# Where an expert's down weights are rounded, and how the second copy of the expert sums is added

## The chip, the cores and the metric

The kernel runs on one core of one Trainium2 chip. The metric is the device time of one execution in microseconds; lower is better. An execution of the kernel is profiled once beside the timed runs, and all rows below come from that one execution.

## What is computed

One encoder block over 1024 positions of 1024 channels: a token mixing part (spatial gating and a Fourier mix), then a mixture of experts, then a final norm. The change touches the expert part and the end. Cut to what matters:

```python
def step(y, blk):                       # one block: up to 128 rows of one expert
    tok, gate, e = blk
    xb = x_pad[tok]                     # 128 x 1024
    h = silu(xb @ w_gate[e]) * (xb @ w_up[e])      # 128 x 256
    out = (h @ w_down[e]) * gate[:, None]          # 128 x 1024
    return y.at[tok].add(out), None
y, _ = lax.scan(step, y0, blocks)       # 64 experts, top 8 of them for each of 1024 rows
h = h + routed + shared
return rms_norm(h, final_norm_g)
```

Everything is float32. Each expert brings 3 MB of weights (gate, up and down, 1 MB each).

## The kernel before

The rows that an expert has to work on are cut into **items** of 128 rows; the inputs here give 93 items for 64 experts, and experts with two items mostly alternate with experts that have one. Items run one after the other, three to a pass of the loop (`TURN = 3`).

Products are made with rounded operands in two parts: a weight tile is split into a **high** part (rounded by ScalarE, ACT: `split_gu` and `split_dn`, lines 959 and 963) and a **rest** (what is left, taken off by VectorE, DVE: `rest_gu` and `rest_dn`, lines 1203 and 1210). Three products of the parts then stand for one. Gate and up weights are split in two pieces (`GU_PARTS = 2`, one is gate and one is up, 128x2048 each), down weights in two of 128x1024 (`KF = 2`). Activations are split in the same way: `xTh` and `xTl` from the transposed rows, `hTh` and `hTl` from the transposed middle rows.

What TensorE (PE) does in item i, in order: the 8 transposes of item i+1's rows (L464), the 12 down products of item i-1 (L744, which need its `w_dn` and `hTl`), 2 transposes of item i's middle rows (L752, which need `hh`), and the 24 gate and up products of item i+1 (L730, which need `w_gu`, `xTh` and `xTl`). I give times in an item from its **T**, the start of its L464 transposes; the last of the 24 products is followed at once by the next T.

What ACT does in item i: the silu `hs` (L969), `xTh` (L974), the first piece of the gate and up weights for item i+2 if that item opens a new expert, `hTh` (L984), the copy `ob` of item i-1's result (L980), the second piece, and last the down weights for item i+1 if that item opens an expert. DVE: `hh` (L1367), `xTl` (L1374), the rest of item i's own down weights (ACT has rounded them one item before), `hTl` (L1379), and both gate and up rests for item i+2. An expert's weights are split once, in the items around its first block; the flags `now`, `coming` and `ahead` say whether item i, i+1 or i+2 is such a first block.

Loads are issued by SyncE (SP) from one instruction stream. There are two raw buffers for gate and up and two for down, one expert in each:

```python
load_next_gu(t * 2 + 1, 0)     # waits until expert j-2 is split on ACT and DVE, then issues
gu_landed(1, t + 1)            # waits for the other buffer's load, then tells ACT (s_rg)
load_next_dn(t * 2, 1)
dn_landed(0, t)                # tells ACT of down weights (s_rd)
```

So the word that expert j-1's gate and up weights have landed comes to ACT only behind the issue of expert j's load, which waits for expert j-2's split to be done.

Results of items are added to rows in HBM with an indirect accumulating DMA from GpSimd (POOL, L1583), in two copies, `yv` and `yv2`. The last three items are not stored: at the end their rows are added by one-hot products (L786). For the end, SP loads the first copy in 8 chunks of 128 rows into `ya_in` (L452), and POOL adds the second copy to each chunk with an accumulating DMA (L1642). DVE then adds the one-hot products to a chunk (L1457, two halves), ACT squares it, POOL makes the root, DVE scales it (L1467), and SP stores it (L455).

Of the kernel before, what the change touches and what calls it, by code (L numbers as in the profile page):

```python
# [23 lines left out]
P = 128  # L24
D = 1024
# [37 lines left out]
def build(nc, x, g1, w_in, ln_g, ln_b, wsT, bsT, ga, gb, w_out, g2, w_router, rbias, wg, wu, wd,  # L63
          sg, su, sd, dft_pos, dft_ch, gf, out, hn_d, y_d):
    ctx = ExitStack()
    with ctx:
        top = [nc.sbuf_base]

        def place(name, shape, dt, at=None):
# [6 lines left out]
            if at is None:  # L76
# [136 lines left out]
        ob_rest = [place("ob_rest0", [P, D], F32R, Z_AT + 12 * KB), place("ob_rest1", [P, D], F32R, S_AT + 12 * KB),  # L213
                   place("ob_rest2", [P, D], F32R, T_AT)]
        tok_row = place("tok_row", [P, S], F16, M_AT + KB)
# [57 lines left out]
        s_yl = [sem(f"y_last_in{c}") for c in range(NC)]  # L273
        s_oh, s_obh, s_obl = sem("onehot_ready"), sem("last_results_high"), sem("last_results_rest")
        s_tok, s_col = sem("token_row"), sem("last_slot_columns")
        s_lastmm, s_sum = sem("last_rows_done"), sem("last_rows_added")
# [51 lines left out]
        def _(sp):  # L328
# [122 lines left out]
            for c in range(NC):  # L451
                sp.dma_start(ya_in[:, c, :], yv[c]).then_inc(s_x[c], 16)  # L452
            for c in range(NC):
                sp.wait_ge(s_of, c + 1)
                sp.dma_start(out_v[c], ya_in[:, c, :]).then_inc(s_ost, 16)  # L455
# [370 lines left out]
        def _(act):  # L826
# [166 lines left out]
            def item(i, u, turn, coming, final=False):  # L993

                silu(i)
                if final:
                    if u + 1 < TURN:
                        evac_xT(i + 1)
                    evac_h(i)
                    evac_out(i - 1, (u - 1) % TURN, turn if u else turn - 1)  # L1000
# [18 lines left out]
                with act.If(coming[0] > 0):  # L1019
                    act.wait_ge(s_rd, coming[1] + 1)  # L1020
                    split_dn(coming[2])
                return ahead

            def turn_of_items(turn, final=False):
                coming = expert(turn * TURN + 1)
                for u in range(TURN):
                    coming = item(turn * TURN + u, u, turn, coming, final and u > 0)
# [32 lines left out]
        def _(dv):  # L1060
# [327 lines left out]
            def item(i, u, now, coming, final=False):  # L1388
# [14 lines left out]
                if isinstance(i, int) and i == 0:  # L1403
# [47 lines left out]

            def add_last(c):
                dv.wait_ge(s_yl[c], 16)
# [5 lines left out]

            add_last(0)  # L1460
            add_last(1)
            dv.wait_ge(s_gf, 16)
# [9 lines left out]
        def _(gp):  # L1472
# [162 lines left out]
            for c in range(NC):  # L1635
                gp.wait_ge(s_x[c], 48)
                if c == 0:
# [61 lines left out]
```

## Time and profile before

| | us |
|---|---|
| median of 3 runs | 1382.69 (1381.22 to 1388.32) |
| the profiled execution, device time | 1384.51 |
| span of the profiled execution, first to last instruction | 1382.8 |
| PE busy | 1321.7 (96%) |
| DVE busy | 859.0 (62%) |
| ACT busy | 722.8 (52%) |
| POOL busy | 521.9 (38%) |

The profiled execution took 1.8 us more than the median, and 1.7 us of its device time lie around the span. About 900 us of the span are the expert loop, and the last 50 us or so are the end. A share of busy time is an average over stages; what bounds one stage is read from its waits.

### The profile page before, as it was taken

The numbers are of one execution on the slowest core, as the hardware profiler recorded it, in microseconds if no ns is written. First come the engines' busy times: TensorE is split into PE (matmuls) and PEld (weight loads), VectorE is DVE, ScalarE is ACT, GpSimd is POOL, SyncE is SP. The second block draws the span as 40 slices with busy tenths as digits, with TensorE's granted clock in tenths as the row PEclk, the third lists the DMA queues.
The fourth block names the chain that finished last, engine by engine and source line by source line (L and its number), as shares of the span: only waits on it lengthen the run. The fifth ranks groups of instructions, "written<-read, shape, count | busy, mean of one in ns | idle before, by whom it ended". The sixth has DMA issues, their size and how long they took to land.

```text
span 1382.8 us, 25986 instructions
## 1 busy us (share of the span) xinstructions
PE 1321.7 (96%) x6030; PEld 1033.6 (75%) x6032; DVE 859.0 (62%) x1203; ACT 722.8 (52%) x916; POOL 521.9 (38%) x610
## 2 busy tenths in 40 slices
PE   6999988999999999999999999999999999999996
PEld 5885465888445787888878887888778888888875
DVE  5430544355585667667766767667676767667766
ACT  5320244211002667676766657676666766676752
POOL 2431201000002444545444444444454444444562
PEclk9999998999899999999999999999999999999998
DMA  9604032011046799999999999999999999999979
GB/s 338 190 13 164 0 121 92 31 46 46 9 183 217 258 313 345 282 325 305 334 299 326 314 297 350 287 337 315 313 315 320 315 337 308 298 332 306 334 213 249
DMA packets 88306, 338.02 MB, mean 244 GB/s; under 512 B 12496, under 2 KB 23760, under 8 KB 71504
## 3 DMA queue, kind: packets, MB, share of 16 engines
q1 hardware_dynamic: 60624, 250.53, 47.2%
q0 software_dynamic: 27648, 87.06, 27.8%
q8 instruction: 18, 0.29, 0.1%
q14 instruction: 16, 0.13, 0.0%
HBM read 288.99 MB, written 65.27 MB: 256 GB/s over the span
## 4 chain that ended last, share of the span: by engine, by line
PE 57%; DVE 9%; DMA 9%; issue 9%; ACT 5%; SPq 5%; DVEq 4%; ACTq 1%; POOL 0%; POOLq 0%
PE ps L730 18%; PE ps L615 7%; PE ps L481 7%; PE ps_out L744 6%; DMA raw_dn<-in_w_down 5%; DVE w_gu L1203 5%; PE ps L650 4%; PE ps L517 4%; PE ps L464 4%; SPq L318 3%; DMA ya_in<-y_rows_dram 2%; ACT w_gu L959 2%; DVE w_dn L1210 2%; PE ps L566 2%; DVEq L318 2%
## 5 line engine op out<-in xcount | busy, mean ns | idle before, releaser
L730 PE MATMUL ps<-w_gu,xTh 128*128 x1488 | 468.6, 396 | 17.8 <-DVE xTl L1374 15.5
L730 PEld LDWEIGHTS ps<-w_gu,xTh 128*128 128x128 f32 x1488 | 273.8, 188 | 81.4 <-issue 27.1
L1583 POOL DMA_INDIRECT y_rows_dram<-ob,idxs x90 | 222.3, 2470 | 235.2 <-ACT ob L980 213.7
L1203 DVE TENSOR_TENSOR w_gu<-raw_gu,w_gu (+1 forms) x128 | 290.4, 2287 | 11.9 <-issue 11.8
L730 PE MATMUL ps<-w_gu,xTl 128*128 x744 | 291.1, 391 | 0.0
L959 ACT ACTIVATE w_gu<-raw_gu (+1 forms) x128 | 245.7, 1920 | 70.8 <-SPq L404 70.8
L744 PE MATMUL ps_out<-w_dn,hTh 128*128 x744 | 242.1, 407 | 1.6 <-ACT ob L980 1.6
L963 ACT ACTIVATE w_dn<-raw_dn (+1 forms) x128 | 128.2, 1053 | 87.3 <-SPq L408 78.4
L730 PEld LDWEIGHTS ps<-w_gu,xTl 128*128 128x128 f32 x744 | 139.7, 188 | 28.3
L1374 DVE TENSOR_TENSOR xTl<-ps,xTh 128x512 fp32r<-128x512 f32 x186 | 119.8, 686 | 59.5 <-ACT xTh L974 58.2
L744 PEld LDWEIGHTS ps_out<-w_dn,hTh 128*128 128x128 f32 x744 | 133.2, 189 | 27.0 <-issue 1.9
L1210 DVE TENSOR_TENSOR w_dn<-raw_dn,w_dn (+1 forms) x128 | 150.4, 1216 | 1.8 <-ACT w_dn L963 1.8
L744 PE MATMUL ps_out<-w_dn,hTl 128*128 x372 | 146.0, 392 | 0.0
L1557 POOL DMA_INDIRECT Xg<-hn_rows_dram,idxg x94 | 100.2, 1066 | 76.5 <-POOL idxg L1554 74.4
L974 ACT ACTIVATE xTh<-ps 128x512 fp32r<-128x512 f32 x186 | 101.3, 602 | 39.5 <-PE ps L464 39.5
L1367 DVE SCALAR_TENSOR_TENSOR hh<-hs,gate,ps 128x256 f32<-128x256 f32 x93 | 44.4, 477 | 119.9 <-ACT hs L969 119.9
L1505 POOL TENSOR_SCALAR rs<-ms 128x1 f32<-128x1 f32 x40 | 21.1, 527 | 230.4 <-ACT junk L829 229.2
L464 PEld LDWEIGHTS ps<-ident,Xg 128*128 128x128 f32 x744 | 96.9, 190 | 8.0 <-issue 0.5
L1567 POOL COPY gate<-Xg 128x1 f32 x93 | 41.1, 442 | 159.9 <-DVE hh L1367 102.2
L464 PE MATMUL ps<-ident,Xg 128*128 128x128 f32 x744 | 97.3, 274 | 0.0
L980 ACT ACTIVATE ob<-ps_out 128x1024 f32<-128x1024 f32 x92 | 94.1, 1023 | 0.0
L1379 DVE TENSOR_TENSOR hTl<-ps,hTh 128x256 fp32r<-128x256 f32 x93 | 39.0, 419 | 84.9 <-ACT hTh L984 84.9
(241 smaller groups left out, 1608.0 us busy)
## 6 DMA issues: line engine op xcount, KB each, us to landing
raw_gu<-in_w_gate SPq DMA_DIRECT2D x64, 1024.0 KB
raw_gu<-in_w_up SPq DMA_DIRECT2D x64, 1024.0 KB
raw_dn<-in_w_down SPq DMA_DIRECT2D x64, 1024.0 KB
y_rows_dram<-zero SPq DMA_DIRECT2D x1, 4608.0 KB, 20.0
x_ring<-in_x SPq DMA_DIRECT2D x8, 512.0 KB, 4.7
w_in_sb<-in_w_in SPq DMA_DIRECT2D x8, 512.0 KB, 9.9
xh<-in_x SPq DMA_DIRECT2D x8, 512.0 KB, 7.3
w_out_sb<-in_w_out SPq DMA_DIRECT2D x1, 4096.0 KB, 13.1
```

The lines of the kernel that those rows point to most:

```text
L464: last = pe.transpose(ps[banks[k // 4]][:, (k % 4) * P:(k % 4 + 1) * P], src[:, k:D:KD], ident[:, :])
L481: mm = pe.matmul(ps[2 + 2 * (c % 2) + half][:, :], x_[:, c % 2, k, :], w_, start=(k == 0 and n == 0), stop=(k == KD - 1 and n == 2))
L730: mm = pe.matmul(ps[3][:, :], x_[:, k, :], w_gu[:, bass.ds(at, 1), part, :, k, :], start=(k == 0 and part == 0 and x_ is xTh), stop=(k == ...
L744: mm = pe.matmul(ps[6 + half][:, :], h_[:, k, :], w_dn[:, bass.ds(at, 1), part, k, half * 512:(half + 1) * 512], start=(k == 0 and part == ...
L959: act.activation(gu_part(w_gu[:, :, 0, :, :, :], at, m), gu_part(raw_gu, at, m), ACT.Copy).then_inc(s_hg, 1)
L963: act.activation(w_dn[:, bass.ds(at, 1), 0, k, :], raw_dn[:, bass.ds(at, 1), k, :], ACT.Copy).then_inc(s_hd, 1)
L974: act.activation(xTh[:, half * 4:half * 4 + 4, :], ps[1 + half][:, :].rearrange("p (k t) -> p k t", k=4), ACT.Copy).then_inc(s_xa, 1)
L1203: dv.tensor_tensor(gu_part(w_gu[:, :, 1, :, :, :], at, m), gu_part(raw_gu, at, m), gu_part(w_gu[:, :, 0, :, :, :], at, m).bitcast(F32), AL ...
L1210: dv.tensor_tensor(w_dn[:, bass.ds(at, 1), 1, k, :], raw_dn[:, bass.ds(at, 1), k, :], w_dn[:, bass.ds(at, 1), 0, k, :].bitcast(F32), ALU.s ...
L1374: dv.tensor_tensor(xTl[:, part, :], ps[1 + half][:, :].rearrange("p (k t) -> p k t", k=4), xTh[:, part, :].bitcast(F32), ALU.subtract).the ...
L1557: gp.indirect_dma_start(out=Xg[:, u, :], out_offset=None, in_=hn_d[:, :], in_offset=bass.IndirectOffsetOnAxis(ap=idxg[:, u:u + 1], axis=0) ...
L1583: gp.indirect_dma_start(out=y_d[:, :], out_offset=bass.IndirectOffsetOnAxis(ap=idxs[:, u:u + 1], axis=0), in_=ob[:, u, :], in_offset=None, ...
```

## The change

In the expert loop, on ACT an item now rounds **its own** down weights (flag `now`) where it opens an expert, between the copy `ob` and the second piece of gate and up; before, the down weights of the next item (`coming`) were rounded at the item's end. On DVE the first gate and up rest now comes right behind `xTl`, ahead of `hTl`; then `hTl`, the down rest, and the second gate and up rest.

At the end, the second copy of chunks 0 to 3 is loaded by SP as a plain load into a new tile `yb_in`, in the place of the raw down weights, and added to `ya_in` by DVE (`both_copies`); POOL adds chunks 4 to 7 only. The tile `ob_rest0` moves out of the way of `yb_in`.

```diff
@@ SP, the end
             for c in range(NC):
                 sp.dma_start(ya_in[:, c, :], yv[c]).then_inc(s_x[c], 16)
+            sp.wait_ge(s_hd, NE * KF)
+            sp.wait_ge(s_ld, NE * KF)
+            for c in range(NC // 2):
+                sp.dma_start(yb_in[:, c, :], yv2[c]).then_inc(s_x[c], 16)
@@ ACT item
                 if not (isinstance(i, int) and i == 0):
                     evac_out(i - 1, (u - 1) % TURN, turn if u else turn - 1)
+                if not (isinstance(i, int) and i == 0):
+                    with act.If(now[0] > 0):
+                        act.wait_ge(s_rd, now[1] + 1)
+                        split_dn(now[2])
                 with act.If(ahead[0] > 0):
                     split_gu(ahead[2], (1,))
-                with act.If(coming[0] > 0):
-                    act.wait_ge(s_rd, coming[1] + 1)
-                    split_dn(coming[2])
@@ DVE item
                 else:
+                    with dv.If(ahead[0] > 0):
+                        rest_gu(ahead[2], ahead[1], (0,))
+                    rest_h(i)
                     with dv.If(now[0] > 0):
                         rest_dn(now[2], now[1])
-                if not (isinstance(i, int) and i == 0):
-                    rest_h(i)
-                with dv.If(ahead[0] > 0):
-                    rest_gu(ahead[2], ahead[1], range(GU_PARTS))
+                    with dv.If(ahead[0] > 0):
+                        rest_gu(ahead[2], ahead[1], (1,))
@@ DVE, the end
+            def both_copies(c):
+                dv.wait_ge(s_x[c], 64)
+                dv.tensor_tensor(ya_in[:, c, :], ya_in[:, c, :], yb_in[:, c, :], ALU.add).then_inc(s_both, 1)
...
+            both_copies(0)
+            both_copies(1)
             add_last(0)
+            both_copies(2)
             add_last(1)
+            both_copies(3)
@@ POOL, the end
-            for c in range(NC):
+            for c in range(NC // 2, NC):
                 gp.wait_ge(s_x[c], 48)
```

The order on ACT in one item of the loop, before (the branches skip a split where its flag is not set):

```order
L984 ACTIVATE hTh<-ps 128x256
L980 ACTIVATE ob<-ps_out 128x1024
L1017 COMPARE_AND_BRANCH
L959 ISA x2
L959 ACTIVATE w_gu<-raw_gu 128x2048
L1017 UNCONDITIONAL_BRANCH
L1019 COMPARE_AND_BRANCH
L1020 ISA
L963 ISA
L963 REGISTER_ALU
L963 ACTIVATE w_dn<-raw_dn 128x1024
```

and now:

```order
L992 ACTIVATE hTh<-ps 128x256
L988 ACTIVATE ob<-ps_out 128x1024
L1027 COMPARE_AND_BRANCH
L1028 ISA
L971 ISA
L971 REGISTER_ALU
L971 ACTIVATE w_dn<-raw_dn 128x1024
...
L1030 COMPARE_AND_BRANCH
L967 ISA x2
L967 ACTIVATE w_gu<-raw_gu 128x2048
```

The two down pieces moved from behind the second gate and up piece to ahead of it, and belong to the item itself. On DVE, in one item before:

```order
L1374 TENSOR_TENSOR xTl<-ps,xTh 128x512
L1410 COMPARE_AND_BRANCH
L1209 ISA
L1210 ISA x2
L1210 TENSOR_TENSOR w_dn<-raw_dn,w_dn 128x1024
...
L1379 TENSOR_TENSOR hTl<-ps,hTh 128x256
L1414 REGISTER_ALU
L1414 COMPARE_AND_BRANCH
L1202 ISA
L1203 ISA x2
L1203 TENSOR_TENSOR w_gu<-raw_gu,w_gu 128x2048
```

and now:

```order
L1384 TENSOR_TENSOR xTl<-ps,xTh 128x512
L1422 REGISTER_ALU
L1422 COMPARE_AND_BRANCH
L1212 ISA
L1213 ISA x2
L1213 TENSOR_TENSOR w_gu<-raw_gu,w_gu 128x2048
L1422 UNCONDITIONAL_BRANCH
L1389 TENSOR_TENSOR hTl<-ps,hTh 128x256
...
L1220 TENSOR_TENSOR w_dn<-raw_dn,w_dn 128x1024
...
L1213 TENSOR_TENSOR w_gu<-raw_gu,w_gu 128x2048
```

One gate and up piece moved ahead of `hTl`, and the down rests now stand behind it, ahead of the second piece.

## Rows read from the trace of the kernel before

**Rows 1.** The waits of all engines, 450 to 1322 us: total, times, longest
```profile
ACT w_gu L959 <- SPq L404: 70.8, 34, 4.2
PE ps L730 <- DVE xTl L1374: 15.5, 27, 1.3
```

**Rows 2.** The same view for SP's own queue, 450 to 1322 us
```profile
SPq L391 <- DVE w_gu L1203: 169.0, 61, 7.2
...
SPq L404 <- DMA raw_gu<-in_w_up: 6.9, 2, 6.7
```

**Rows 3.** Busy time by window: us, PE, PEld, DVE, ACT, POOL, clock, DMA share, GB/s
```profile
1200.00:1300.00 100.00, 98.59 (x478) 81.43 (x477) 71.25 (x72) 68.51 (x82) 47.73 (x52) 1.00 1.00 323
```

**Rows 4.** Timeline of PE, starts of items (T): start us, us, engine line op
```profile
466.79 0.93 PE L464 MATMUL ps<-ident,Xg 128*128 128x128 f32 x7
...
631.60 1.04 PE L464 MATMUL ps<-ident,Xg 128*128 128x128 f32 x8
...
640.99 1.05 PE L464 MATMUL ps<-ident,Xg 128*128 128x128 f32 x8
...
650.45 1.04 PE L464 MATMUL ps<-ident,Xg 128*128 128x128 f32 x8
...
654.96 0.50 PE L730 MATMUL ps<-w_gu,xTh 128*128 x1 [0.44 <-issue]
...
660.53 1.05 PE L464 MATMUL ps<-ident,Xg 128*128 128x128 f32 x8
...
1330.74 0.71 PE L464 MATMUL ps<-ident,Xg 128*128 128x128 f32 x5
```

**Rows 5.** Timeline of ACT, the same three items and one item later
```profile
633.66 1.92 ACT L959 ACTIVATE w_gu<-raw_gu  x1
...
636.89 1.92 ACT L959 ACTIVATE w_gu<-raw_gu  x1
...
645.03 1.92 ACT L959 ACTIVATE w_gu<-raw_gu  x1 [1.86 <-SPq L404]
...
648.01 1.92 ACT L959 ACTIVATE w_gu<-raw_gu  x1
649.82 2.00 ACT L963 ACTIVATE w_dn<-raw_dn  x2
...
684.16 1.92 ACT L959 ACTIVATE w_gu<-raw_gu  x1 [2.32 <-SPq L404]
```

**Rows 6.** Timeline of DVE, the same three items and two later places
```profile
634.52 2.35 DVE L1210 TENSOR_TENSOR w_dn<-raw_dn,w_dn  x2
...
637.12 4.49 DVE L1203 TENSOR_TENSOR w_gu<-raw_gu,w_gu  x2
...
643.41 1.29 DVE L1374 TENSOR_TENSOR xTl<-ps,xTh 128x512 fp32r<-128x512 f32 x2 [1.32 <-ACT xTh L974]
647.24 0.42 DVE L1379 TENSOR_TENSOR hTl<-ps,hTh 128x256 fp32r<-128x256 f32 x1 [2.55 <-ACT hTh L984]
647.90 4.59 DVE L1203 TENSOR_TENSOR w_gu<-raw_gu,w_gu  x2 [0.24 <-issue]
...
653.47 1.29 DVE L1374 TENSOR_TENSOR xTl<-ps,xTh 128x512 fp32r<-128x512 f32 x2 [0.58 <-ACT xTh L974]
...
678.97 2.29 DVE L1203 TENSOR_TENSOR w_gu<-raw_gu,w_gu  x1
...
710.35 0.47 DVE L1367 SCALAR_TENSOR_TENSOR hh<-hs,gate,ps 128x256 f32<-128x256 f32 x1
710.90 1.29 DVE L1374 TENSOR_TENSOR xTl<-ps,xTh 128x512 fp32r<-128x512 f32 x2
```

**Rows 7.** The chain that ended last, 640 to 700: start us, us, what
```profile
686.41 12.28 DMA raw_dn<-in_w_down
```

**Rows 8.** Timeline of DVE, the end of the kernel
```profile
1354.95 3.68 DVE L1457 TENSOR_TENSOR ya_in<-ps,ya_in 128x512 f32<-128x512 f32 x6 [4.66 <-PE ps L786]
...
1377.31 1.28 DVE L1467 SCALAR_TENSOR_TENSOR ya_in<-ya_in,rs,gf_row 128x1024 f32<-128x1024 f32 x1 [0.77 <-POOL rs L1507]
```

More of the change, by code:

```diff
@@ L212, in build @@
         ob_high = place("ob_high", [P, TURN, D], F32R, X_AT)
-        ob_rest = [place("ob_rest0", [P, D], F32R, Z_AT + 12 * KB), place("ob_rest1", [P, D], F32R, S_AT + 12 * KB),
+        ob_rest = [place("ob_rest0", [P, D], F32R, X_AT + 12 * KB), place("ob_rest1", [P, D], F32R, S_AT + 12 * KB),
                    place("ob_rest2", [P, D], F32R, T_AT)]
+        yb_in = place("yb_in", [P, NC // 2, D], F32, Z_AT)
         tok_row = place("tok_row", [P, S], F16, M_AT + KB)
@@ L271, in build @@
         s_hg, s_lg, s_hd, s_ld, s_hl = (sem(n) for n in ("gu_high", "gu_rest", "down_high", "down_rest", "hT_rest"))
-        s_yl = [sem(f"y_last_in{c}") for c in range(NC)]
+        s_yl = {c: sem(f"y_last_in{c}") for c in range(NC // 2, NC)}
         s_oh, s_obh, s_obl = sem("onehot_ready"), sem("last_results_high"), sem("last_results_rest")
         s_tok, s_col = sem("token_row"), sem("last_slot_columns")
+        s_both = sem("copies_summed")
         s_lastmm, s_sum = sem("last_rows_done"), sem("last_rows_added")
@@ L452, in _ @@
                 sp.dma_start(ya_in[:, c, :], yv[c]).then_inc(s_x[c], 16)
+            sp.wait_ge(s_hd, NE * KF)
+            sp.sem_inc(s_turn_sp, 1)
+            sp.wait_ge(s_ld, NE * KF)
+            sp.sem_inc(s_turn_sp, 1)
+            for c in range(NC // 2):
+                sp.dma_start(yb_in[:, c, :], yv2[c]).then_inc(s_x[c], 16)
             for c in range(NC):
@@ L991, in expert, with item @@
                 return act.snap(both % 2, min_val=0, max_val=1), e, place_of(act, e)
-            def item(i, u, turn, coming, final=False):
+            def item(i, u, turn, now, coming, final=False):
                 silu(i)
@@ L999, in item @@
                     evac_h(i)
-                    evac_out(i - 1, (u - 1) % TURN, turn if u else turn - 1)
+                    evac_out(i - 1, (u - 1) % TURN, turn)
                     if u + 1 < TURN:
-                        with act.If(coming[0] > 0):
-                            act.wait_ge(s_rd, coming[1] + 1)
-                            split_dn(coming[2])
+                        for flag, e, at in (now, coming):
+                            with act.If(flag > 0):
+                                act.wait_ge(s_rd, e + 1)
+                                split_dn(at)
                     return coming
@@ L1016, in item @@
                     evac_out(i - 1, (u - 1) % TURN, turn if u else turn - 1)
+                if not (isinstance(i, int) and i == 0):
+                    with act.If(now[0] > 0):
+                        act.wait_ge(s_rd, now[1] + 1)
+                        split_dn(now[2])
                 with act.If(ahead[0] > 0):
                     split_gu(ahead[2], (1,))
-                with act.If(coming[0] > 0):
-                    act.wait_ge(s_rd, coming[1] + 1)
-                    split_dn(coming[2])
                 return ahead
             def turn_of_items(turn, final=False):
-                coming = expert(turn * TURN + 1)
+                now, coming = expert(turn * TURN), expert(turn * TURN + 1)
                 for u in range(TURN):
-                    coming = item(turn * TURN + u, u, turn, coming, final and u > 0)
+                    now, coming = coming, item(turn * TURN + u, u, turn, now, coming, final and u > 0)
             act.wait_ge(s_rg, 1)
@@ L1408, in item @@
                         rest_gu(coming[2], coming[1], range(GU_PARTS))
-                else:
+                    with dv.If(ahead[0] > 0):
+                        rest_gu(ahead[2], ahead[1], range(GU_PARTS))
+                else:
+                    with dv.If(ahead[0] > 0):
+                        rest_gu(ahead[2], ahead[1], (0,))
+                    rest_h(i)
                     with dv.If(now[0] > 0):
                         rest_dn(now[2], now[1])
-                if not (isinstance(i, int) and i == 0):
-                    rest_h(i)
-                with dv.If(ahead[0] > 0):
-                    rest_gu(ahead[2], ahead[1], range(GU_PARTS))
+                    with dv.If(ahead[0] > 0):
+                        rest_gu(ahead[2], ahead[1], (1,))
                 return ahead
```

7 lines of the change are left out of this document (5 added, 2 removed).

## The prediction

> **What bounds the kernel now.** I read the windows first. In the expert loop PE is busy 98.6 of 100 us at a granted clock of 1.00, and the DMA engines show a share of 1.00 at 323 GB/s [rows 3], so two things could set the pace. The waits decide. What PE waits for in the loop is `xTl` from DVE, 27 times and 15.5 us [rows 1]; ACT waits for SP's word that gate and up weights have landed, 34 times and 70.8 us [rows 1]; but SP itself waited for a landing of `raw_gu` only twice, 6.9 us, against 61 waits and 169.0 us for DVE's gate and up rests [rows 2]. So the word is late because it stands behind the next load in SP's stream, and that load waits for DVE. The pace is set by PE and by a loop DVE, SP, ACT, DVE around it, not by landings.
>
> Then I read three items in a row. Going through the timeline, the 89 items from T = 466.79 to 1330.74 (864.0 us, 9.71 each) [rows 4] fall in three kinds. An X item opens an expert and has gate and up weights to split for a later one (28 items); a Y item has only gate and up (27); a Z item has only down weights (28). In six places, about 16 items apart, three experts with one item each follow one another: there a W item, with both kinds of weights like X, stands between Y and Z. X, Y and W together are the 61 items behind SP's 61 waits [rows 2]. The six places can be found in the chain of work, where each leaves a piece of 11.7 to 13.8 us of the down weights' load; one stands here [rows 7].
>
> X starts at 631.60 and takes 9.39, Y at 640.99 takes 9.46, Z at 650.45 takes 10.08 [rows 4]. X's 9.39 is the floor: PE never waits in it. In X, DVE's gate and up rests end at 637.12 + 4.49 = 641.61, 0.62 into Y (I call this the **spill**) [rows 6]. In Y, ACT can begin its first piece only at 645.03, after 1.86 us of waiting for SP, 3.42 behind the end of DVE's work for X; its second piece starts at 648.01, 2.98 later, and the down weights run until 651.8, 1.4 into Z [rows 5]. DVE's rests for Y end at 652.49, 2.04 into Z; the last of them (2.29) starts 0.27 after ACT's second piece ended [rows 5, 6]. In Z this makes `xTl` start at 653.47, 3.02 after T; the first gate and up product comes at 654.96, 1.49 later, and the next T 5.57 after that [rows 4, 6]. So an item lasts 5.57 + 1.49 + the start of its `xTl`, and never less than 9.39; `xTl` may start as late as 2.33 at no cost.
>
> **X after the change.** DVE has the same work, but what it may begin has changed. ACT's first piece stays at 2.06 and ends at 3.98 [rows 5]. DVE's first rest follows at 4.25 and ends at 6.54 (2.29), `hTl` (0.42) ends at 6.96, the down rests (2.35 for two) at 9.31 [rows 6]. On ACT the down weights now take the place at 5.29 where the second piece stood; they hold the engine 1.9 (2.00, less an overlap of 0.1), so the second piece runs from 7.18 to 9.10, and DVE's last rest from 9.37 to 11.66. The spill into Y is 2.27 where it was 0.62: 1.65 later. PE needs the down weights for its down products at about 10.3 (next T plus 0.9, most of the 8 transposes' 1.04 [rows 4]), and they are ready at 9.31, so X itself costs nothing; if that 1.0 us of cover were gone, PE would wait in 28 items.
>
> **Y.** `hs` is ready early here, so `hh` starts as the spill ends and `xTl` 0.55 behind it, as at 710.35 and 710.90 [rows 6]. That gives `xTl` at 2.82 and an item of 9.88 (+0.4). Queued behind DVE's late rest is SP's wait for it, then the word to ACT: ACT's first piece moves from 4.04 to 2.27 + 3.42 = 5.69, the second to 8.67, ends 10.59, and DVE's last rest runs 10.86 to 13.15. The earlier place of the first rest buys nothing here, since the last one follows ACT's second piece either way. ACT no longer rounds down weights at the end of Y, so `hs` of Z is freed by 0.7 to 1 us; but `hh` waits for DVE, whose spill into Z is now 13.15 - 9.88 = 3.27 instead of 2.04, and that is what is late next.
>
> **Z.** `xTl` at 3.82, an item of 10.88 (+0.8 on 10.08). ACT and DVE split its down weights between 5.3 and 9, with no spill.
>
> **W and the Z behind it.** W gets the spill of 3.27: 10.88 long. Between DVE's end and ACT's first piece lie 684.16 - (678.97 + 2.29) = 2.90 in W [rows 5, 6], so ACT starts at 6.17; DVE's first rest 8.36 to 10.65, `hTl` 11.07, the down rests 13.42, the last rest (ACT's second piece ends 12.96) 15.71. PE would begin the down products at 10.88 + 0.9 = 11.8 and waits 1.6 us for down weights: a wait that rows of before do not have. The spill is 4.83, `xTl` 5.38, and this Z takes 12.44. In exchange the six 12 us pieces of the down load [rows 7] leave the chain, since the weights are wanted five or six us later than before, and the X behind is at its floor.
>
> **Sum of the loop.** 28 X of 9.39 (262.9), 27 Y of 9.88 (266.8), 22 Z of 10.88 (239.4), 6 W of 10.88 (65.3), 6 Z of 12.44 (74.6): 909 against 864.0, which is +45. Taking 0.47 instead of 0.55 behind the spill (the overlap of 710.35 with the rest before it) lowers 61 items by 0.08 each, to +40. I take +42. The extra branches and register instructions of the second `If` run ahead on the sequencers while the engines are behind; they are nothing as long as an engine has queued work, and at most 0.2 us in each of 61 items (12 us) if not. The loads start later by the same amounts as they are wanted later, and cost nothing more.
>
> **The end.** DVE starts its adds at 1354.95 after 4.66 us of waiting for PE, and has 3 chunks in 3.68, 1.23 each; the last scaling ends at 1378.59 [rows 8]. The change adds four adds of 128x1024, 1.18 each by the down rests (2.35 for two) [rows 6]. Two of them fit in the 4.66 us if their data is there. Without any wait DVE would then end at 1354.95 + 8 x 1.23 + 2 x 1.18 + 8 x 1.27 = 1377.3: 1.3 less than now, because VectorE's work is the bound once the accumulating DMA is not. On the other side, the four plain loads (2.1 MB, 6.5 us at 323 GB/s [rows 3]) queue behind 4.2 MB of the first copy and share the engines with the accumulates, and `add_last(0)` is queued behind the first two sums; if they come 3 us late the end comes 3 us late. I take 0, with bounds of -1.3 and +3.
>
> Against the profiled execution (1384.5) the sum gives 1426.5; it took 1.8 us more than the median, so against the median 1382.7 it is 1424.7, rounded to 1425.
>
> **Rivals.** *The word to ACT does not move* (A). If the landings, not SP's order, set when ACT starts in Y, DVE's lateness in X is absorbed there. Then Y costs +0.4, Z loses its late `hs` and falls to 9.48 (`xTl` at the 2.42 of 643.41 [rows 4, 6]), W too, and the Z behind W stays at 12.4 because of the down weights: 262.9 + 266.8 + 208.6 + 56.9 + 74.6 = 870, or 1389. For it speaks the DMA share of 1.00 [rows 3], against it SP's two waits for landings [rows 2]. The same result, near no change, comes out if the memory traffic paces the loop: the bytes are the same, the loop would keep its 864 us and the kernel end at 1381 to 1386. The Trainium skill (SBUF — State Buffer, A bandwidth-pool intuition that's wrong) says that HBM is almost always the end-to-end bottleneck, with about 358 GB/s for a core. By that rule the loop at 323 GB/s would be close to the limit and the order of the splits would not matter; the trace bears it out only in part, since SP waited for its buffers and not for data.
>
> *Faster* (B). The place is Z: with the down weights gone from Y's end, `hs` is on time and `xTl` can start at its 2.42. It decides itself at the end of DVE's last rest in X: if that stays within about 1.8 us of the next item (I work out 2.27), Y and Z both fall to about 9.5, W and its Z too, and the loop takes 28 x 9.39 + 61 x 9.48 = 841, 23 less, or 1360. For it speaks that DVE idles 2.55 us before `hTl` in Y [rows 6]; against it, that ACT's second piece cannot end before 9.1 in X by its own row durations.
>
> *Worse than forecast* (C). Down weights are now split in the item before their product. If the word `s_rd` or the load comes late (12.3 us from issue to landing [rows 7], with some 14 us at hand behind a W), or PE waits in X too, each such wait goes to PE in full; 1 us in 34 items is +34, or 1459.
>
> **Chances.** Forecast (1400 to 1442) 0.72; A 0.10; B 0.08; C 0.10. The range takes in A's upper end and the lower part of C and leaves out about 2 in 10: 1388 to 1445. About 0.5% (1375.8 to 1389.6) is what a measurement of this kernel can tell from no change; faster 0.09, same 0.09, slower 0.82.
>
> **What would show it.** Right: ACT's second gate and up piece in X starts near 7.2 and DVE's last rest ends 2.3 into Y; ACT's wait for SP in Y grows to about 3.5 us each; Y, Z near 9.9 and 10.9; a new wait of PE's down products for `w_dn` on DVE, six times 1.6 us; PE's wait for `xTl` about three times its 15.5 us; at the end DVE with hardly a gap and no gain. Wrong: ACT's first piece in Y still 4.0 after T (A), Z at 9.5 (B), many waits of ACT for `raw_dn` (C).

## The result, and the profile after

The changed kernel takes 1402.92 us (median, 1400.61 to 1403.26) where the kernel before took 1382.6 in the same comparison: 1.013 times as long, 95% interval 1.011 to 1.015, or +20.3 us. The forecast was +42, in a range from 1388 to 1445. The measured time lies inside that range, but the size was twice too large, and the table below shows that the loss does not sit where the forecast had most of it.

The profiled execution spans 1401.0 us (before 1382.8). From the first T to the last, the loop takes 1350.35 - 466.95 = 883.4 us where it took 864.0 [rows 4]: +19.4. What lies behind the last T is 1.4 us shorter. So the loop carries the whole loss.

The three items of [rows 4 to 6], in the changed kernel: X starts at 635.28, Y at 644.66, Z at 654.48, the next at 664.37 (timeline of PE; the first and the last row are the loop's ends).

```profile
466.95 1.04 PE L472 MATMUL ps<-ident,Xg 128*128 128x128 f32 x8
...
635.28 1.04 PE L472 MATMUL ps<-ident,Xg 128*128 128x128 f32 x8
...
644.66 1.04 PE L472 MATMUL ps<-ident,Xg 128*128 128x128 f32 x8
...
648.90 0.73 PE L738 MATMUL ps<-w_gu,xTh 128*128 x2 [0.18 <-DVE xTl L1384]
...
654.48 1.04 PE L472 MATMUL ps<-ident,Xg 128*128 128x128 f32 x8
...
664.37 1.04 PE L472 MATMUL ps<-ident,Xg 128*128 128x128 f32 x8
...
1350.35 1.05 PE L472 MATMUL ps<-ident,Xg 128*128 128x128 f32 x8
```

ACT and DVE in the same items (timeline):

```profile
640.57 2.00 ACT L971 ACTIVATE w_dn<-raw_dn  x2
642.46 1.92 ACT L967 ACTIVATE w_gu<-raw_gu  x1
...
649.16 1.92 ACT L967 ACTIVATE w_gu<-raw_gu  x1 [1.63 <-SPq L406]
```

```profile
644.82 2.29 DVE L1213 TENSOR_TENSOR w_gu<-raw_gu,w_gu  x1 [0.31 <-issue]
647.03 0.47 DVE L1377 SCALAR_TENSOR_TENSOR hh<-hs,gate,ps 128x256 f32<-128x256 f32 x1
647.42 1.28 DVE L1384 TENSOR_TENSOR xTl<-ps,xTh 128x512 fp32r<-128x512 f32 x2
...
654.50 2.29 DVE L1213 TENSOR_TENSOR w_gu<-raw_gu,w_gu  x1 [0.44 <-ACT w_gu L967]
656.71 0.47 DVE L1377 SCALAR_TENSOR_TENSOR hh<-hs,gate,ps 128x256 f32<-128x256 f32 x1
657.28 1.29 DVE L1384 TENSOR_TENSOR xTl<-ps,xTh 128x512 fp32r<-128x512 f32 x2
```

In X everything stands where the forecast had it: the second piece on ACT at 642.46 - 635.28 = 7.18, the last rest over at 647.11, 2.45 into Y (forecast 2.27), `xTl` 2.76 into Y, an item of 9.82. Then it parts from the forecast: ACT's first piece in Y starts at 649.16, 2.05 behind the end of DVE's rest, and not 3.42. Its second piece, DVE's last rest and `hh` are earlier too, the last rest by 1.0 (9.84 into Y and not 10.86), and Z takes 9.89 and not 10.88.

Going through all 89 items:

| kind, count | before, mean us | forecast | after | after, against forecast in sum |
|---|---|---|---|---|
| X, 28 | 9.56 | 9.39 | 9.39 | 0 |
| Y, 27 | 9.47 | 9.88 | 10.17 | +8 |
| Z, 22 | 10.00 | 10.88 | 9.73 | -25 |
| W, 6 | 10.10 | 10.88 | 9.87 | -6 |
| Z behind W, 6 | 10.00 | 12.44 | 12.11 | -2 |

Against before, the forecast put its 45 us mainly into Z (+19), the Z behind W (+15) and Y (+11). Measured are Y +19, the Z behind W +13, X -5, Z -6 and W -1. So Z and W, which were to lose 24 us, became shorter. Two of the means hide two groups each. Of the 27 Y, 17 take 9.81 to 9.85 and 10 take 10.65 to 11.13; of the six Z behind W, four take 11.3 to 11.5 and two 13.6, so that their mean comes near 12.44 is in part luck.

The waits from 450 to 1322 us, which answer to [rows 1] (all engines, then SP's queue: total, times, longest):

```profile
ACT w_gu L967 <- SPq L406: 60.8, 31, 4.2
...
PE ps L738 <- DVE xTl L1384: 24.1, 41, 1.4
...
PE ps_out L752 <- issue: 7.4, 6, 2.0
```

```profile
SPq L393 <- DVE w_gu L1213: 150.6, 55, 7.1
```

PE's wait for `xTl` grew from 15.5 to 24.1 us, and the new wait ahead of the down products is there six times. The view names no engine for it, but in all six places these products start 0.2 to 0.3 us after DVE's last down rest ends. ACT waits for SP no longer than before, 60.8 against 70.8. For the first piece in Y it starts later and waits less. All its waits for SP's word on down weights are gone, as are SP's waits for landings [rows 2]. In the view of before these waits of ACT are longer in total than the 70.8 us for gate and up weights that the prediction reads:

```profile
ACT w_dn L963 <- SPq L408: 78.4, 24, 6.1
```

The end of the kernel, timeline of DVE, which answers to [rows 8]:

```profile
1370.02 2.35 DVE L1467 TENSOR_TENSOR ya_in<-ya_in,yb_in 128x1024 f32<-128x1024 f32 x2
...
1395.84 1.28 DVE L1491 SCALAR_TENSOR_TENSOR ya_in<-ya_in,rs,gf_row 128x1024 f32<-128x1024 f32 x1 [0.77 <-POOL rs L1531]
```

From the last T to the last scaling's end are 1397.12 - 1350.35 = 46.8 us, before 1378.59 - 1330.74 = 47.9. Once the first of the last rows were there, DVE ran without a wait for data, and the lower bound of -1.3 was nearly reached.

### The profile page after: what moved, and what is told of

Its sections match the earlier page's. It is cut to its first block, busy times and chain, and to the rows that moved or that the text cites. A ratio compares the mean times of both kernels' runs of the same rounds, so it can differ in the third digit from the quotient of the medians.

```text
span 1401.0 us, 26297 instructions
## 1 busy us (share of the span) xinstructions
PE 1325.1 (95%) x6030; PEld 1034.2 (74%) x6032; DVE 865.9 (62%) x1207; ACT 727.7 (52%) x916; POOL 474.0 (34%) x606
## 4 chain that ended last, share of the span: by engine, by line
PE 67%; DVE 10%; issue 8%; ACT 5%; DVEq 5%; ACTq 2%; SPq 2%; DMA 1%; POOL 0%; POOLq 0%
PE ps L738 22%; PE ps_out L752 11%; PE ps L623 6%; PE ps L489 6%; PE ps L472 4%; PE ps L658 4%; PE ps L525 4%; DVEq L320 3%; DVE w_dn L1220 3%; DVE w_gu L1213 3%; PE ps L574 2%; ACT w_dn L971 2%; ACT w_gu L967 2%; DVE xTl L1384 1%; PE ps L668 1%
## 5 line engine op out<-in xcount | busy, mean ns | idle before, releaser
L967 ACT ACTIVATE w_gu<-raw_gu (+1 forms) x128 | 245.2, 1917 | 67.7 <-SPq L406 62.4
L1607 POOL DMA_INDIRECT y_rows_dram<-ob,idxs x90 | 167.6, 1862 | 242.2 <-ACT ob L988 233.5
L1591 POOL COPY gate<-Xg 128x1 f32 x93 | 64.3, 692 | 218.1 <-PE ps L472 106.9
L977 ACT ACTIVATE hs<-ps 128x256 f32<-128x256 f32 x93 | 35.8, 385 | 134.4 <-PE ps L738 134.4
L1529 POOL TENSOR_SCALAR rs<-ms 128x1 f32<-128x1 f32 x40 | 20.3, 506 | 236.9 <-ACT junk L837 235.8
L752 PEld LDWEIGHTS ps_out<-w_dn,hTl 128*128 128x128 f32 x372 | 70.2, 189 | 16.5
```

Of the source, the lines that this page charges most:

```text
L752: mm = pe.matmul(ps[6 + half][:, :], h_[:, k, :], w_dn[:, bass.ds(at, 1), part, k, half * 512:(half + 1) * 512], start=(k == 0 and part == ...
L967: act.activation(gu_part(w_gu[:, :, 0, :, :, :], at, m), gu_part(raw_gu, at, m), ACT.Copy).then_inc(s_hg, 1)
L1607: gp.indirect_dma_start(out=y_d[:, :], out_offset=bass.IndirectOffsetOnAxis(ap=idxs[:, u:u + 1], axis=0), in_=ob[:, u, :], in_offset=None, ...
```

## The experiments

All times are medians with their ratio to the kernel before, run on the same chip, and its 95% interval. The runs used three chips, on which the kernel before took 1382.3 to 1383.9 us. "The loop" is the time from the first to the last T of the 89 items, and lengths of items are means; each comes from one profiled execution.

### The two halves of the change

`loop_only` has the reordered splits and the old end, `end_only` the new end and the old loop.

> The change's reordering of the splits in the loop on ACT and DVE, with the end of the kernel as before. Theory 1 (the loop carries the whole loss, through DVE's last rest in X, which ends 1.8 us later in Y, and the PE waits that follow; the end gained 1.4): last L464 transposes at about +19.5 against before, device time +19 to +21, 1402 to 1404, a little slower than the changed kernel by 0.5 to 1.5 us. Theory 2 (the end costs, and its plain loads disturb the last items): +15 or less. Theory 3 (the two parts need each other: the later loads of down weights run into the end): something else than the sum of this run and the one with the end alone.

> Before, with only the new end: half of the second copy as plain loads by SP into yb_in and added on DVE. Theory 1: the end is bound by DVE's adds and scalings in both versions, so -1.4 us, between 0 and -2 (1381 to 1383). Theory 2 (plain loads behind the first copy come late and hold the queued adds): 0 to +3. In the trace DVE's four new adds take 1.2 us each, two of them inside DVE's wait for PE.

Measured: `loop_only` 1403.15, 1.013 (1.010 to 1.016), loop 884.5; `end_only` 1380.63, 0.998 (0.996 to 0.9995), DVE's last scaling ends 46.6 behind the last T, 1.3 sooner than before. The loop alone carries the loss. The changed kernel was to be 0.5 to 1.5 us faster than `loop_only` and is not measurably so. In the trace of `loop_only` the old end takes 46.0 us behind the last T, less than the 46.8 of the new end in the changed kernel; DVE waits for data only once there, 0.73 us, where it waited three times, 3.2 us, in the kernel before. So the end's gain shows only behind the old loop; what the new end is worth behind the changed one is not shown.

### Take the lag away in the kernel before

Two edits on SP. `look_first`:

```diff
             def load_next_gu(j, at):
+                e = look(sp, 2, j, NE - 1)
                 sp.wait_ge(s_hg, (j - 1) * GU_PARTS)
...
                 sp.wait_ge(s_lg, (j - 1) * GU_PARTS)
...
-                load_gu(sp, look(sp, 2, j, NE - 1), at)
+                load_gu(sp, e, at)
```

`word_first`:

```diff
-                load_next_gu(t * 2 + 1, 0)
                 gu_landed(1, t + 1)
+                load_next_gu(t * 2 + 1, 0)
...
```

The other two places where a load is followed by such a word are changed in the same way.

> Before, with one edit: in load_next_gu SP loads the expert's number into its register ahead of its two waits and not behind them. It tests the step of the prediction that took the 3.42 us from DVE's last rest to ACT's first piece in Y as fixed: in the trace of before 1.50 us of it is this one register load, which takes 0.28 in the changed kernel at the same place. Theory 1 (the register load is part of the path): ACT's first gate and up piece in Y starts at 2.1 to 2.6 after T instead of 4.04, its wait for SP falls from 70.8 us in sum to below 30, Z's xTl starts at 2.4 instead of 3.02, Z takes 9.4 to 9.5: 28 items x 0.5 = -14, time 1366 to 1371. Theory 2 (whatever slows the register load holds SP's next instruction just as long, the issue of the load or the word): ACT's start stays within 0.3 us of 4.04 and the time within 2 us of before. Theory 3 (landings set it): same, with SP's wait for a landing in place of the register load.

> Before, with the word that expert j-1's gate and up weights have landed given to ACT ahead of the issue of expert j's load, so that it no longer stands behind SP's wait for DVE's rests. It tells order from landing, rival A of the prediction. Theory 1 (order on SP sets ACT's start in Y): ACT's first piece in Y starts at 2.1 instead of 4.04, no wait of ACT for SP in Y, DVE's rests of Y end near 9.5 after T, Z's xTl starts at 2.4, Z 9.4 to 9.5; the whole loop at its floor of 9.4 an item would be -28 us, I expect -14 to -26 (1357 to 1369). Theory 2 (rival A, landings or the memory traffic): SP waits for raw_gu instead, 2 us in each Y, and the time stays within 0.3% of before (1379 to 1387).

Measured: `look_first` 1385.31, 1.001 (0.999 to 1.003), and `word_first` 1384.55, 1.0005 (0.999 to 1.002). No change, so neither gain of theory 1 came, and yet its mechanism is there: in `look_first` ACT's first piece in Y starts at 2.68 (median of 27) instead of 4.01, in `word_first` at 2.05. In `look_first` Y is 9.44, and Z falls from 10.00 to 9.37, 18 us less in Z and W together. X takes it back: in `look_first` from 9.38 to 9.77, behind a W from 10.22 to 12.52, 22 us more; in `word_first` the X behind a W takes 13.56. The waits of ACT and of SP's queue, and a piece of the chain, in `look_first`:

```profile
ACT w_dn L964 <- SPq L409: 100.2, 27, 7.8
...
ACT w_gu L960 <- SPq L405: 16.1, 23, 3.5
```

```profile
SPq L409 <- DMA raw_dn<-in_w_down: 62.4, 27, 4.0
```

```profile
528.55 13.79 DMA raw_dn<-in_w_down
```

ACT's wait for gate and up weights went from 70.8 to 16.1 us, its wait for down weights from 78.4 to 100.2, and SP now stands 62.4 us (before 11.4) in waits for down weights to land. So the kernel before sits against two limits that are close together: the order on SP, and behind it the landing of down weights, which its order of splits wants early.

`word_half` and `before_half` load half of the down weights, to tell traffic from order:

```diff
-                load_dn(sp, look(sp, 2, j, NE - 1), at)
+                load_half_dn(sp, look(sp, 2, j, NE - 1), at)
```

> The kernel before with the word first, and only half of the down weights loaded (128x1024 of 128x2x1024 for each expert from the third on; the other half of the tile keeps old numbers, so the down products are not the reference's). 31 MB less are loaded. Theory 1 (with the word first, landings of down weights set the pace): X and the X behind W fall from 9.51 and 13.56 to 9.4, the loop to 836 to 840, the time 1354 to 1360. Theory 2 (the 13.56 come from the order of waits on SP and not from the traffic): within 5 us of 1384.

> The kernel before, in its own order, with only half of the down weights loaded, as in the run with the word first (the down products are not the reference's). Theory 1 (in before the order on SP sets Z's 10.0 and the traffic only the X behind W): Z stays at 10.0, only the X behind W falls from 10.22 to 9.4, 6 x 0.8 = -5 us, 1377 to 1381. Theory 2 (the traffic already sets the pace of before): Z falls to 9.4 as well, 1355 to 1365.

Measured: `word_half` 1360.21, 0.983 (0.981 to 0.985), loop 840.8, X behind W 9.72 instead of 13.56; `before_half` 1378.45, 0.997 (0.995 to 0.998), X behind W 9.38, Z still 9.83. Both come out nearly as theory 1 has it (`word_half` is 0.2 us over its range, and Z in `before_half` 0.2 under). So in the old order the down weights' load costs about 5 us; once the order on SP is mended (`word_first`) it costs 24 (1384.6 against 1360.2). Half a load both moves fewer bytes and lands sooner; these runs do not tell the two apart.

### Put the lag back into the changed kernel

Register loads on SP, behind its wait for DVE's rests, four in `after_lag` and two in `after_lag2`:

```diff
                 sp.wait_ge(s_lg, (j - 1) * GU_PARTS)
                 sp.sem_inc(s_turn_sp, 1)
+                look(sp, 2, j, NE - 1)
+                look(sp, 2, j, NE - 1)
                 load_gu(sp, look(sp, 2, j, NE - 1), at)
```

> The changed kernel, with four more register loads of 0.28 us each on SP between its wait for DVE's rests and the issue of the next gate and up load, so that the lag from DVE's last rest to ACT's first piece in Y, 2.05 us in the changed kernel, comes back to the 3.4 us that the prediction used. Theory 1 (the prediction's chain was right and only this lag was mis-sized): ACT's first piece in Y starts near 5.7 after T, Z and W take 10.6 to 10.9, the Z behind W 12.3 and more; the loop 25 to 34 us longer than that of the changed kernel's 883, the time 1420 to 1436. Theory 2 (something else keeps Z short): the time rises by less than 10 us, under 1413.

> The changed kernel with two more register loads on SP behind its wait for DVE's rests. Four of them moved the issue of the next load by 2.2 us in Y, so two should move it by 1.1 and bring ACT's first piece in Y to 5.6 after T, where the prediction had it (5.69). Theory 1 (this lag is the term that was mis-sized, the rest of the chain stands): Z 10.6 to 10.9, W the same, the Z behind W 12.4 and more; with Y at its measured 10.17 the loop is 263 + 275 + 239 + 65 + 75 = 917, the time 1424 to 1438, the prediction's 1425 or somewhat over. Theory 2 (Z's 9.73 has another reason as well): Z under 10.4, time under 1418.

Measured: `after_lag` 1480.5, 1.070 (1.068 to 1.072); `after_lag2` 1441.2, 1.042 (1.040 to 1.044). One extra look costs 0.55 us, not 0.28, so four of them overshot their expectation by far, and two by 3 us. The lag is the median over the 27 Y items, the lengths are means:

| kernel | lag, DVE's end to ACT's start | Z | W | Z behind W | loop |
|---|---|---|---|---|---|
| changed | 2.05 | 9.73 | 9.87 | 12.11 | 883 |
| the forecast | 3.42 | 10.88 | 10.88 | 12.44 | 909 |
| `after_lag2` | 3.16 | 10.68 | 10.81 | 14.11 | 922 |
| `after_lag` | 4.27 | 11.93 | 12.17 | 14.80 | 962 |

With nearly the forecast's lag Z and W come out at nearly the forecast's lengths. This is what was mis-sized. The Z behind W is then 1.7 us longer than forecast, because W has a lag of its own: in the W items of `after_lag2` ACT starts 4.2 us behind DVE (median of 6), where I took 2.90 and the changed kernel has 2.75.

### Why the lag was 3.4 before and 2.05 after

The register load L318 (L320 after the change) of SP, between DVE's last rest of X and the issue for the next expert: in the kernel before, around 642 us, and in the changed kernel around 647 (view by source line: count, least/median/most ns).

```profile
L318 SPq TENSOR_LOAD <-tab x2: 266/884/1503, 641.8 to 645.0; - x2
```

```profile
L320 SPq TENSOR_LOAD <-tab x2: 268/272/277, 647.3 to 649.1; - x2
```

1503 against 277 ns is 1.2 of the 1.4 us. It is the same in all 27 Y items: this load takes 1.17 to 1.53 us before and 0.26 to 0.46 after, while the stretch from DVE's end to the load (0.19) and from the load to the issue (0.39) did not change. POOL's timeline (before, then after) shows what stands ahead of it:

```profile
637.86 3.03 POOL L1583 DMA_INDIRECT y_rows_dram<-ob,idxs  x1 [2.08 <-ACT ob L980]
```

```profile
641.54 1.85 POOL L1607 DMA_INDIRECT y_rows_dram<-ob,idxs  x1 [2.34 <-ACT ob L988]
```

Before, the register load starts 3.9 us behind the issue of the indirect store of result rows, after the change 5.8 us behind it (in both kernels the median of the 27 as well). Two runs changed the store:

> The kernel before, with the indirect store of result rows writing instead of accumulating (so sums over experts are missing from the output). It asks what makes SP's register load at the start of Y take 1.5 us in before, at a time when for 1 us and more only the packets of the indirect accumulate run. Theory 1 (the accumulating packets slow it): the longest register loads of SP fall from 1.5 to under 0.6 us, ACT's first piece in Y starts near 2.9 instead of 4.04, Z falls below 9.6, and with less traffic the time is 1355 to 1370. Theory 2 (any burst of the indirect queue, or something else, slows it): loads of 1 us and more remain, Z stays near 10, the time within 10 us of before by the lighter traffic alone.

> The kernel before without the indirect stores of result rows (POOL raises the semaphore itself; the sums over experts are missing from the output). In five traces, with the store accumulating or writing, a register load of over 0.42 us is found only in the stretch from 2 to 7 us behind the issue of such a store. Theory 1 (the store's packets slow the loads): not one register load over 0.42 us in the loop, ACT's first piece in Y near 2.6 to 2.9 after T. Theory 2 (it is the gather, or the engines' own crowd of loads around T): loads of 0.6 us and more remain.

Measured: `before_noacc` 1359.08, 0.982 (0.981 to 0.984); `before_nostore` 1356.39 in one run, the spans 1360.2 and 1354.7. SP's register loads from 450 to 1322 us, before, writing without accumulating, and without the store:

```profile
L318 SPq TENSOR_LOAD <-tab x123: 174/276/1529, 459.5 to 1318.0; - x123
```

```profile
L318 SPq TENSOR_LOAD <-tab x123: 262/280/1658, 458.3 to 1296.2; - x123
```

```profile
L318 SPq TENSOR_LOAD <-tab x123: 263/268/289, 459.9 to 1288.6; - x123
```

Without the store not one of 730 register loads in the loop, on any engine, takes over 0.33 us, and the lag is 2.05 us, the same as in the changed kernel. GpSimd's gathers are still issued in that run, so they alone do not slow a load; theory 2 of `before_nostore` falls.

`before_noacc` is less clear-cut. Loads up to 1.66 us remain, so a store that only writes slows register loads too, against theory 1. But three of theory 1's four signs came: the time, Z at 9.41, and ACT's first piece at 2.92. At the place that counts, SP's load in Y, it is 0.27 to 0.52 us (before 1.17 to 1.53), and the lag is 2.20. So accumulating does matter for how slow the load at this place is. That the store that only writes is over sooner (the DMA share fell from 0.97 to 0.85) would explain it, but is not shown.

It is the store that slows the register loads of PE, ACT, DVE and SP, and the change moved SP's load past the stretch in which it does. Whether its packets do it or something else in its handling was not told apart. `before_nostore` also has a loop of 834.8, every kind of item at 9.38 or 9.39: the old order reaches the floor too, where the store and its traffic are gone (DMA share 0.70).

### Why Y was 10.17

In 10 of 27 Y items `xTl` starts at 3.56 to 4.04 and not at 2.76 to 2.78 (13 of them was my count ahead of the run below). The chain of the changed kernel at such a place, with Y's T at 714.46:

```profile
714.79 0.12 issue
...
715.02 1.06 DVEq L320
...
717.30 0.09 DVE hh L1377
717.39 0.03 issue
717.42 0.30 DVEq L320
```

The pass of three items begins here, and DVE reads its three flags from the table, one of them in 1.06 us, ending 4.7 us behind the issue of a store. In all ten, one of the three takes 0.94 to 1.32 us. `after_late_look` moves the three register loads behind `hh` and `xTl`:

```diff
                 gated_h(i, u)
+                if look_now:
+                    rest_xT(i + 1)
+                    now, coming = look_now()
+                    ahead = expert(i + 2)
...
```

> The changed kernel, with DVE's three register loads at the start of a pass of the loop moved behind hh and xTl of the pass's first item. In 13 of the 27 Y items, where the pass begins with Y, xTl starts at 3.68 and not 2.76, and the item takes 10.7 and not 9.8. Theory 1 (the register loads stand open there, because DVE comes to the start of the pass with no work queued): xTl falls to 2.8 and these Y to 9.8; but Z behind them has taken 9.38 and not 9.9, so part comes back: loop -4 to -12, the time 1391 to 1399. Theory 2 (the branch at the loop's end or the fetch of its code is what takes the 0.9 us): Y unchanged, 1401 to 1405.

Measured: 1397.15, 1.010 (1.007 to 1.014); loop 878.8, Y 9.92, the longest Y 10.27 instead of 11.13, Z unchanged at 9.74. Theory 1, at the low end of its gain, since the Z behind W grew from 12.11 to 12.60. Most of the term's excess over 9.88 was these looks.

### Take the waits out of the changed kernel

`after_word` is `word_first` on the changed kernel. `after_pe` regroups the 24 products, so that the rest operands are wanted later; `after_word_pe` has both:

```diff
-                pe.wait_ge(s_lg, (e + 1) * GU_PARTS)
-                pe.wait_ge(s_xd, 2 * i + 2)
-                for k in range(KD):
-                    for x_, part in ((xTh, 0), (xTh, 1), (xTl, 0)):
+                pe.wait_ge(s_xa, 2 * i + 2)
+                for x_, part in ((xTh, 0), (xTl, 0), (xTh, 1)):
+                    if x_ is xTl:
+                        pe.wait_ge(s_xd, 2 * i + 2)
+                    if part:
+                        pe.wait_ge(s_lg, (e + 1) * GU_PARTS)
+                    for k in range(KD):
...
```

> The changed kernel, with the word that gate and up weights have landed given to ACT ahead of the issue of the next load. In the loop of before this moved 18 us out of Z and W and 22 us into X, because the down weights were not there. Theory 1 (the changed order asks for down weights 5 to 6 us later, so the memory traffic has room, and only VectorE's late rest in X is left): Z, W and the Z behind W fall to 9.4, Y stays at 9.8, X at 9.4: 28 x 9.39 + 27 x 9.85 + 34 x 9.4 = 849 for the loop, 34 less than the changed kernel, 1366 to 1374 us, which beats both kernels. Theory 2 (the memory traffic sets the loop's time in every order, 864 us at 312 GB/s): 1380 to 1386, with the waits in X or before the down products.

> The changed kernel, with one edit on PE: the 24 gate and up products run as 8 of xTh with the high weights, 8 of xTl with the high weights, 8 of xTh with the rest weights, and each group waits for its own operand. xTl may then start 1.9 us later at no cost, at 4.2 instead of 2.33. Theory 1 (DVE's late rest costs only through xTl): Y, whose xTl starts at 2.76 or 3.68, falls to 9.4, Z and W too, the Z behind W to 10.4; the loop 83 x 9.38 + 6 x 10.4 = 841, the time 1358 to 1366. Theory 2 (the memory traffic sets a floor, 322 GB/s is the highest that 100 us showed): the loop no lower than 845, with new waits for landings, 1362 to 1380. Theory 3 (the regrouped products are slower by themselves): X above 9.4.

> The changed kernel with both edits, the word to ACT ahead of the next load's issue and the three groups of products. Theory 1: every item at 9.38, the loop 835 to 842, the time 1352 to 1360. Theory 2 (memory traffic): the loop 845 or more, 1362 to 1370, no better than with the products alone.

| kernel | time | ratio (interval) | loop | X | Y | Z | Z behind W |
|---|---|---|---|---|---|---|---|
| `after_word` | 1378.62 | 0.997 (0.995 to 0.998) | 860.6 | 9.40 | 10.19 | 9.38 | 9.96 |
| `after_pe` | 1375.22 | 0.995 (0.993 to 0.996) | 855.5 | 9.38 | 9.39 | 9.40 | 12.73 |
| `after_word_pe` | 1352.19 | 0.978 (0.976 to 0.979) | 835.0 | 9.38 | 9.39 | 9.38 | 9.38 |

`after_word` came out 5 to 12 us over its expectation, by the looks of the section above (Y 10.19) and the spill into the Z behind W. `after_pe` came out 9 us over its theory 1, its loop 14. It left the six places behind W: ACT's pieces there still wait for SP, so the down weights come late, and PE waits for them:

```profile
PE ps_out L754 <- DVE w_dn L1222: 15.6, 6, 2.8
```

With both edits every kind of item is at its floor, and the windows view from 450 to 1330 us has PE busy 876.9 of 880 us (before, then `after_word_pe`; last columns clock, DMA share, GB/s):

```profile
450.00:1330.00 880.00, 861.40 (x4161) 710.83 (x4160) 612.38 (x613) 586.34 (x700) 420.29 (x451) 1.00 0.97 312
```

```profile
450.00:1330.00 880.00, 876.90 (x4286) 730.23 (x4285) 634.97 (x632) 601.23 (x716) 406.57 (x466) 1.00 0.98 322
```

This version beats both kernels: 30 us less than before, and about 50 less than the changed one, which was timed in another comparison. The same edits on the kernel before, the grouped products alone (`before_pe`) and with the word first (`word_pe`), tell what the change's order is worth there:

> The kernel before with the three groups of products alone. Z's xTl at 3.02 would no longer cost. Theory 1 (down weights land too late for before's order): Z falls to 9.4 as in the kernel with the look first, and X and the X behind W take it back; loop 855 to 866, the time 1375 to 1386. Theory 2: loop 845 or less, under 1366.

> The kernel before with the word first and the three groups of products: the changed kernel with both edits, but for the order of the splits (and the end, worth 3 us). It tells what the change's order is worth once the two waits that it makes late are gone. Theory 1 (before's order needs an expert's down weights 5 to 6 us earlier than they can land; that is where the kernel with the word first lost, 13.56 in X behind W): X behind W 12 to 14, the loop 855 to 866 against 835, the time 1375 to 1386. Theory 2 (the three groups alone make the gain): loop 835 to 840, the time 1352 to 1360, and the change's order is worth nothing.

Measured: `before_pe` 1373.09, 0.992 (0.990 to 0.995), loop 854.9, X behind W 10.77, the Z behind W 10.44; `word_pe` 1394.84, 1.008 (1.006 to 1.011), loop 875.2, X 10.52 and behind W 11.64. `before_pe` is better than expected, `word_pe` is worse even than expected. In `word_pe` the waits of ACT and of SP's queue are:

```profile
ACT w_dn L965 <- SPq L408: 154.3, 33, 7.7
```

```profile
SPq L404 <- DMA raw_gu<-in_w_up: 427.7, 58, 10.1
...
SPq L408 <- DMA raw_dn<-in_w_down: 64.1, 32, 3.0
```

SP now stands in the wait for gate and up weights to land, and the issue of the down load queues behind it: in Z it is issued 8.1 us after T in the median, in `look_first` 6.2. The old order needs those weights at Z's end and waits 154 us for them; the changed order needs them in the middle of X. So with the same two edits the changed order is worth 1394.8 - 1352.2 = 43 us, 40 of them in the loop.

## Why the prediction was right and wrong

**Right.** That X stays at its floor while DVE's last rest ends 2.3 us into Y (2.45); `xTl` and the 9.88 of Y where no pass begins (9.82); the down weights as the new wait behind W, six times; the six long pieces of the down load gone from the chain; the end near the lower of its bounds of -1.3 and +3 (-1.1 to -1.4, where I took 0). That the whole loss is in the loop was right too, but not how it is spread over the items.

**The step that failed** is in the part on Y: "ACT's first piece moves from 4.04 to 2.27 + 3.42 = 5.69". It carried over a lag from the trace of before as if it were a property of the chain DVE, SP, ACT. It was 2.05 after the change, and ACT's first piece came at 4.51, 1.2 us ahead of the forecast. This put the 27 items behind a Y at 9.73 (Z) and 9.87 (W) instead of 10.88 and took 31 us out of the sum. The 3.42 was made up of waits and instructions that the view of waits does not list: 1.50 of it was one register load, which is 0.27 elsewhere in the same trace. `after_lag2` shows that with the lag at 3.16 Z takes 10.68, and `before_nostore` that in the old order the lag is 2.05 once the store is gone.

**A term that was too small** is Y: 10.17, not 9.88, +8 us. I held the extra register instructions at "nothing as long as an engine has queued work". DVE's looks at a pass's start were there before as well, but then `xTl` still started within its 2.33 us of room or 0.15 past it; with the later spill they stand open on the path. The 0.2 us for the new register instructions had no row behind it; what stood open here are old ones, and they move `xTl` by 0.8 to 1.3 us at each of ten places. `after_late_look` brings Y to 9.92.

**What bounds the kernel** was half right. I read from [rows 2] that SP waits for its buffers and not for data, and concluded that landings do not set the pace. They hardly do in the kernel as it was (5 us in `before_half`), but they stood close behind: taking the order's wait away alone brought nothing. The hint was in the views of before and was left out: ACT's 78.4 us of waits for down weights, more than the 70.8 for gate and up, and SP's six waits of 11.4 us for their landing. The Trainium skill (SBUF — State Buffer, A bandwidth-pool intuition that's wrong) holds that HBM is almost always the end-to-end bottleneck. These runs agree only in part: the loop at 312 GB/s was bound by order, and the fastest version ran at 322 GB/s with PE at its floor. Halving the down weights' load brought 5 us in the order of before and 24 in that of `word_first`.

**The rivals.** A, the word that does not move, did not come true as such: ACT's start in Y did move, from 4.04 to 4.5. But its consequence for Z (9.48) did for the most part, by another cause. B's threshold, a spill within about 1.8 us, was not met in X. C did not show: X stayed at 9.39, and ACT had no wait for down weights.

## What to carry to other kernels

A gap between two engines that goes through a third one's instruction stream is not a constant: take it apart, instruction by instruction, register loads too, before carrying it to a new place in time, and take as the other bound the sum with each instruction at its usual length. Here that would have been 3.42 - 1.50 + 0.27 = 2.19; the smallest whole lag in a Y of before, 2.84, would not have shown it. When a wait is taken away and the time stays, look at which wait grew by as much (here ACT's for down weights); a change that looks like a loss by itself, later use of late data, can be what makes the next edit pay. Ask of every operand of a long group of products when it is first needed: regrouping the products, at no cost of their own (X stays at 9.38), gave `xTl` 1.9 us more room, and the weights' rests are needed later as well.

## What the runs showed of the hardware

- A register load from SBUF (TENSOR_LOAD) takes 0.27 to 0.32 us in the median on every engine. On PE, ACT, DVE and SP it takes 0.5 to 1.7 us for many of those that end about 3 to 7 us behind the issue of an indirect store of 128 rows of 4 KB (POOL's own take at most 0.35). In the kernel before and in the changed one, all loads over 0.5 us in the loop end 3.1 to 6.1 us behind such an issue. This held whether the store accumulates (1529 ns at most on SP) or writes (1658), and in the loop without the store no load took over 0.33 us, with the gathers still there. What it is in the store that does it stays open, and so does why the plain loads beside it, which keep the DMA share near 1.00, do not.
- One added look, a register load with its register instructions, costs SP's stream 0.55 us, not the 0.28 of the load.
- From 450 to 1330 us the kernel before moved 312 GB/s at a DMA share of 0.97 and `after_word_pe` 322 at 0.98. With half the down weights gone `word_half` moved 282 GB/s while PE was near its floor (loop 840.8 against 835.0), so 322 is what the floor asks for, and whether the chip could give more was not tried.
- At the end DVE, once the first of the last rows were there, did adds, sums and scalings with one gap, 0.77 us; 2.1 MB of plain loads behind 4.2 MB did not hold it up there, and in `end_only` only by 0.89 us, ahead of a wait for PE.
